# A hybrid decoder layer: the LRU's convolution one chunk ahead of its gates, and seven rotating PSUM banks instead of six

## The reference

```python
x = x + 0.5 * rms_norm(swiglu(rms_norm(x, g1), w_gu, w_down), g2)
y = hybrid_mixer(rms_norm(x, mix_pre_g), ...)
x = x + rms_norm(y, mix_post_g)
x = x + 0.5 * rms_norm(swiglu(rms_norm(x, g3), w_gu2, w_down2), g4)

# hybrid_mixer, the recurrent half (512 channels)
xc = causal_depthwise_conv(x_lru, conv_w, conv_b)        # width 4
r = sigmoid(block_diag(xc, w_rg, b_rg)); i = sigmoid(block_diag(xc, w_ig, b_ig))
log_a = 8.0 * r * log_sigmoid(lam); a = exp(log_a)
u = sqrt(-expm1(2 * log_a)) * (i * xc)
h[t] = a[t] * h[t-1] + u[t]
y_lru = h * gelu(gate_lru)
# the other half: attention over a window of 128 keys with a sink per head
y = concat([rms_norm(y_lru, g_lru_out), rms_norm(y_attn, g_attn_out)]) @ w_o
```

## Time and profile before

| | us |
|---|---|
| runs shown, median of 2 | 3468.2 (3390.47 and 3545.94) |
| profiled execution | 3390.16 |
| span of its slowest core, core 7 | 3388.6 |
| spans of all cores | 3377.7 to 3388.6 |
| PE busy, core 7 | 2952.9 (87%), 13,256 matmuls |
| DVE busy | 1545.5 (46%) |
| ACT busy | 1606.7 (47%) |
| mean granted TensorE clock, core 7 | 0.938 |

### The profile page before, as it was taken

The page is one execution under the profiler, slowest core; times in us unless marked ns, Lnnn a source line. Parts: engine busy times, 40 slices in busy tenths (PEclk is TensorE's granted clock), DMA queues, the critical chain, the costliest instruction groups (busy, mean ns, idle before and its releaser), DMA issues.

```text
span 3388.6 us, 41222 instructions; the slowest of 8 cores (3377.7 to 3388.6 us)
## 1 busy us (share of the span) xinstructions
PE 2952.9 (87%) x13256; PEld 1317.4 (39%) x13256; DVE 1545.5 (46%) x2378; ACT 1606.7 (47%) x2376; POOL 504.9 (15%) x744
## 2 busy tenths in 40 slices
PE   6999999999999999999989878777888986876887
PEld 3443444434444444444434323223344432332333
DVE  3255544545445455554555344444422245345252
ACT  3245454464555545555554455356322245445422
POOL 1111111111111111111111111111111110110110
PEclk9999999999999999999999988888899987987988
DMA  8998989899797987979889655565898974754785
GB/s 155 150 150 127 162 136 143 144 135 155 133 148 139 141 150 128 158 136 140 149 129 149 94 93 86 78 100 76 132 153 153 140 106 65 106 88 68 107 142 100
DMA packets 236335, 427.31 MB, mean 126 GB/s; under 512 B 13280, under 2 KB 95456, under 8 KB 236128
## 3 DMA queue, kind: packets, MB, share of 16 engines
q0 software_dynamic: 224320, 382.61, 74.7%
q1 hardware_dynamic: 11808, 42.07, 3.8%
HBM read 798.81 MB, written 8.39 MB: 238 GB/s over the span
## 4 chain that ended last, share of the span: by engine, by line
PE 64%; DVE 13%; ACT 13%; issue 5%; DMA 3%; DVEq 0%; ACTq 0%; SPq 0%; POOLq 0%
PE ps L120 62%; DVE s_y L370 2%; PE ps L124 2%; DVE s_hnm L339 2%; DMA s_xst<-xs 2%; ACT s_sq L301 2%; DVE s_dn L579 2%; DVE s_sg L399 1%; ACT L316 1%; ACT L486 1%; DVE s_xc L456 1%; ACT L397 1%; DVE s_xT L376 1%; DVE s_hseq L499 1%; DMA s_ring<-wgu 1%
## 5 line engine op out<-in xcount | busy, mean ns | idle before, releaser
L120 PE MATMUL ps<-s_hnf,s_ring 128*128 128x512 bf16 x7040 | 1642.6, 392 | 64.8 <-DVE s_hnf L339 35.7
L120 PEld LDWEIGHTS ps<-s_hnf,s_ring 128*128 128x128 bf16 x7040 | 702.7, 101 | 953.4 <-issue 206.4
L120 PE MATMUL ps<-s_act,s_ring 128*128 128x512 bf16 x3520 | 793.1, 382 | 4.1 <-DVE s_act L402 4.1
L399 DVE TENSOR_TENSOR s_sg<-ps,s_sg 128x512 f32<-128x512 f32 x440 | 302.8, 688 | 902.9 <-ACT s_sg L397 813.1
L289 POOL DMA_DIRECT2D s_ring<-wgu x440 | 308.8, 702 | 1590.4 <-PE ps L120 1404.0
L120 PEld LDWEIGHTS ps<-s_act,s_ring 128*128 128x128 bf16 x3520 | 346.1, 98 | 428.0 <-issue 21.1
L397 ACT ACTIVATE s_sg<-ps 128x512 f32<-128x512 f32 x440 | 260.1, 594 | 331.9 <-PE ps L120 295.0
L120 PE MATMUL ps<-s_hnm,s_ring 128*128 128x512 bf16 x1064 | 269.0, 402 | 96.3 <-DVE s_ycat L580 44.9
L402 DVE TENSOR_TENSOR s_act<-ps,s_sg 128x512 bf16<-128x512 f32 x440 | 304.3, 692 | 93.7 <-PE ps L120 62.9
L120 PE MATMUL ps<-s_sq,s_ones 128*128 128x512 bf16 x512 | 188.3, 410 | 105.4 <-ACT s_sq L301 53.3
L350 ACT ACTIVATE s_y<-ps 128x512 f32<-128x512 f32 x160 | 94.7, 592 | 332.0 <-PE ps L120 332.0
(11 more groups left out here) (84 smaller groups left out, 1822.8 us busy)
## 6 DMA issues: line engine op xcount, KB each, us to landing
s_ring<-wgu POOLq DMA_DIRECT2D x440, 512.0 KB, 7.1
s_ring<-wd POOLq DMA_DIRECT2D x160, 704.0 KB, 9.8
s_xst<-xs SPq DMA_DIRECT2D x64, 512.0 KB, 7.4
s_ring<-win POOLq DMA_DIRECT2D x106, 256.0 KB, 5.4
s_ring<-wo POOLq DMA_DIRECT2D x32, 256.0 KB, 4.9
out<-s_xst SPq DMA_DIRECT2D x16, 512.0 KB, 7.8
s_wgb<-wg POOLq DMA_DIRECT2D x1, 256.0 KB, 6.2
s_masks<-masks POOLq DMA_DIRECT2D x1, 96.0 KB, 8.2
```

Source lines behind the costliest of these rows:

```text
L120: return self.e.matmul(*a, **k)
L399: S.add("dve", lambda e, bg=bg, gi=gi: e.tensor_tensor(out=sg[gi][:], in0=ps[bg][:], in1=sg[gi][:], op=ALU.mult), reads=[("ps", bg), ("sg" ...
```

## The change

The LRU is taken apart into `lru_conv(c)` and `lru_gates(c)`. `s_xc` and `s_xcb` get two buffers each, used by even and odd chunks. The convolution and cast of chunk c+1, with its gate projection and Gelu in an output tile, are recorded one step before the gates of chunk c. `s_gl` goes: the Gelu is written straight into `s_ycat`, and the product with the scan is done in place. A chunk now has two steps of side instead of three in the warm-up, three instead of four in an output tile. The output projection no longer squares from PSUM and adds chunk by chunk in bank 6: after its eight copies ACT squares the eight chunks of `s_ycat` from SBUF in a row, and two steps later eight ones matmuls sum them in a rotating bank. Bank 6 joins the rotation: seven banks instead of six in the warm-up, three instead of two for side in the output tiles.

```diff
         def nb():
-            return 4 + nxt("sbank", 2) if bank_mode["split"] else nxt("bank", 6)
+            return 4 + nxt("sbank", 3) if bank_mode["split"] else nxt("bank", 7)
         def nbm():
-            return nxt("mbank", 4) if bank_mode["split"] else nxt("bank", 6)
+            return nxt("mbank", 4) if bank_mode["split"] else nxt("bank", 7)
...
-            for c in range(4):
-                yield from gen_lru_chunk(t, c, own, fl)
+            lru_conv(0, own)
+            yield
+            for c in range(4):
+                if c + 1 < 4:
+                    lru_conv(c + 1, own)
+                yield
+                if own:
+                    yield
+                lru_gates(t, c, own, fl)
+                yield
...
+        def lru_conv(c, own):
+            xc, xcb = xc2[c % 2], xcb2[c % 2]
...
             if own:
                 bgk = proj_chunk(4 + c)
-                S.add("act", lambda e: e.activation(out=gl[:], in_=ps[bgk][:], func=AF.Gelu),
-                      reads=[("ps", bgk)], writes=["gl"])
-            yield
-            yield
-            if own:
-                yield
+                S.add("act", lambda e: e.activation(out=ycat[:, c, :], in_=ps[bgk][:], func=AF.Gelu),
+                      reads=[("ps", bgk)], writes=[("ycat", c)])
+
+        def lru_gates(t, c, own, fl):
...
             yield
-            yield from gen_outproj(oproj, ycat, "ycat", SSB2, "s")
-            yield from gen_residual(par, ycat, "ycat", SSB2, 8, "gh1")
+            for m in range(8):
+                bk = oproj(m)
+                S.add("act", lambda e, m=m, bk=bk: e.activation(out=ycat[:, m, :], in_=ps[bk][:], func=AF.Copy),
+                      reads=[("ps", bk)], writes=[("ycat", m)])
+                yield
+            sis = sumsq_squares(lambda k: ycat[:, k, :], [("ycat", k) for k in range(8)], 8)
+            yield
+            yield
+            ri = sumsq_finish(sis, 1.0 / D)
+            yield from gen_residual(par, ycat, "ycat", None, 8, "gh1", ri=ri)
```

More of the change, by code:

```diff
@@ L186, in build_program @@
         xl = sb("xl", [128, 4, NT + 3], F32)
-        xc = sb("xc", [128, NT], F32)
-        xcb = sb("xcb", [128, NT], BF16)
+        xc2 = [sb("xc%d" % i, [128, NT], F32) for i in range(2)]
+        xcb2 = [sb("xcb%d" % i, [128, NT], BF16) for i in range(2)]
         r_t = sb("r_t", [128, NT], F32)
@@ L364, in gen_outproj, with gen_residual @@
             yield
-        def gen_residual(par, ybuf, ykey, ssb, ghcol, ghkey):
+        def gen_residual(par, ybuf, ykey, ssb, ghcol, ghkey, ri=None):
             xt = xT[par]
-            ri = finish_rstd(ssb, 1.0 / D)
+            if ri is None:
+                ri = finish_rstd(ssb, 1.0 / D)
             for k in range(8):
@@ L445, in gen_lru @@
                 yield
+            lru_conv(0, own)
+            yield
             for c in range(4):
-                yield from gen_lru_chunk(t, c, own, fl)
-        def gen_lru_chunk(t, c, own, fl):
+                if c + 1 < 4:
[7 more added lines that the diff above has]
+            xc, xcb = xc2[c % 2], xcb2[c % 2]
+            kx, kb_ = ("xc", c % 2), ("xcb", c % 2)
@@ L450, in gen_lru_chunk @@
             cw = lambda k: vec[:, V_CONVW + c * 4 + k:V_CONVW + c * 4 + k + 1]
-            S.add(CONV_ENG, lambda e: e.tensor_scalar(out=xc[:], in0=xl[:, c, 3:NT + 3], scalar1=cw(3),
+            S.add("dve", lambda e: e.tensor_scalar(out=xc[:], in0=xl[:, c, 3:NT + 3], scalar1=cw(3),
                                                    scalar2=vec[:, V_CONVB + c:V_CONVB + c + 1], op0=ALU.mult, op1=ALU.add),
-                  reads=[("xl", c), "vec"], writes=["xc"])
+                  reads=[("xl", c), "vec"], writes=[kx])
@@ L454, in gen_lru_chunk @@
             for k in range(3):
[L455 to L464, removed]
@@ L465, in gen_lru_chunk @@
-            S.add("act", lambda e: e.activation(out=xcb[:], in_=xc[:], func=AF.Copy), reads=["xc"], writes=["xcb"])
+                S.add("dve", lambda e, k=k: e.scalar_tensor_tensor(out=xc[:], in0=xl[:, c, k:k + NT], scalar=cw(k),
+                                                                  in1=xc[:], op0=ALU.mult, op1=ALU.add),
+                      reads=[("xl", c), "vec", kx], writes=[kx])
+            S.add("act", lambda e: e.activation(out=xcb[:], in_=xc[:], func=AF.Copy), reads=[kx], writes=[kb_])
@@ L493, in gen_lru_chunk @@
             S.add("dve", lambda e: e.tensor_tensor(out=i_t[:], in0=i_t[:], in1=xc[:], op=ALU.mult),
-                  reads=["i_t", "xc"], writes=["i_t"])
+                  reads=["i_t", kx], writes=["i_t"])
             S.add("dve", lambda e: e.tensor_tensor(out=i_t[:], in0=i_t[:], in1=m_t[:], op=ALU.mult),
@@ L504, in gen_lru_chunk @@
             if own:
-                S.add("dve", lambda e: e.tensor_tensor(out=ycat[:, c, :], in0=hseq[:], in1=gl[:], op=ALU.mult),
-                      reads=["hseq", "gl"], writes=[("ycat", c)])
-            yield
+                S.add("dve", lambda e: e.tensor_tensor(out=ycat[:, c, :], in0=ycat[:, c, :], in1=hseq[:], op=ALU.mult),
+                      reads=["hseq", ("ycat", c)], writes=[("ycat", c)])
         def gen_kv_proj():
```

9 lines of the change are left out of this document (5 added, 4 removed).

## The result

The changed kernel takes 3474.6 us in the median of 11 runs (3450.59 to 3752.28), the kernel before 3394.0 in 10 runs beside them (3387.11 to 3626.14). Some runs of either kernel are up to 300 us longer than the rest, so the medians carry part of that; the ratio, which leaves them out, is 1.0195 with an interval of [1.0172, 1.0217]: slower, by some 66 us. The profiled executions give 3453.06 against 3390.16, 62.9 more.

A forecast was written before the change was run, and what follows sets the result against it. PE was taken as busiest, held by latency in the in-order ACT and DVE queues and by waits for L580. From 3390.2 us, +121 (warm-up), -47 (output tiles) and -16 (output projection) gave 3448, range 3400 to 3500.

The forecast's parts named there:

- within: Whole kernel: time between 3322 and 3458 us, two per cent or 68 us either way; chance 0.52.
- slower: Whole kernel: time above 3458 us, from all of (2) and 0.24 of (1); chance 0.38.
- (1): Whole kernel: the sum holds at 3448 us, with its own range of 3415 to 3485; chance 0.66.
- (2): Output tiles give nothing because ACT is the chain, only the 16 at the ends stay: 3495 us; chance 0.14.
- The warm-up: 12 warm-up tiles: each loses 8.6 us by queue order plus 1.5 of clock, 10.1 a tile, +121 us.
- the chain: Warm-up LRU: ACT and DVE, in order, wait for each other in turn; slot 22's last product comes 9.00 us later.
- The clock term of 1.5: Warm-up tile: PE's clock falls after a wait of some 8 us, now exposed, adding 1.5 us a tile.
- the small waits: Warm-up tile: PE's two waits of 0.57 and 0.40 us after the cast's wait, said to vanish inside the chain.
- The output tiles: Mixer from first scores to third down projection: 125.04 us becomes 114.2, 11.7 gained four times, -47 us.
- The projection: Output projection, ends of stretches: residual and sum a step earlier, FFN norm squares wait less, -16 us, bounds 5 and 21.
- (3): Warm-up loss is hidden because DVE and ACT catch up beside the down projection: 3327 us; chance 0.12.
- (4): Faster: buffer and bank remove PE's waits, 3213 us, if slot 18's sigmoid is not held by chunk 1's cast; chance 0.08.

The follow-up runs named there:

- e2: Changed kernel with the 12 warm-up tiles back in the old order of three steps a chunk; ratio to the kernel before 0.9813, span 3329.5 us.
- e3: Changed kernel with, in the warm-up, only the cast of chunk c+1 moved behind the gates' last exp of chunk c; ratio to the kernel before 0.9817.
- e1: Changed kernel with steps, banks and output projection of before, leaving only the two buffers and the Gelu in place; ratio to the kernel before 1.0002.
- e6: Changed kernel with the old banks, six in the warm-up and two for side in output tiles; ratio to the kernel before 1.0223, span 3476.5 us.
- e9: Changed kernel with the old banks and old output projection, keeping new order, buffers and Gelu in place; no ratio on record, span 3475.6 us.
- e7: Changed kernel with the old LRU steps everywhere, keeping seven and three banks and the new output projection; ratio to the kernel before 0.9994.
- e5: Changed kernel with warm-up convolutions and gates spread over later steps and each later cast behind the previous gates' last exp; ratio to the kernel before 0.9602.
- run 16: Not a follow-up run: words of "then run 16 and 18 matmuls", the matmuls PE ran in two tiles of e7, 3.62 and 4.05 us.

## Why the prediction was right, and where it was wrong

**The step that failed** is "Two per cent, about what a measurement of this kernel can tell". The interval of the ratio is 0.45% wide from end to end, [1.0172, 1.0217], so a change of 1% would have been told from none. My sum stood at +58 us, 1.7%, and I split its case at 3458, ten us above my own number, which put 0.52 into "within" and only 0.38 into "slower": I forecast no change that a measurement could tell, and the runs show one of 1.95%, nine times the 0.22% that the interval reaches to either side. By the measurement's real width nearly all of cases (1) and (2), 0.80, was slower. The sum itself, 3448, stands 5 us below the profiled 3453.06; what failed is the bound by which I turned it into chances. It could have been doubted from the fact that the spans of all eight cores of one execution lie within 11 us, though that doesn't show how runs differ from each other.

**The warm-up: right, by the right cause.** L403 of slot 22 starts 39.50 us after that of slot 16 (898.47 less 858.97); the chain gave 39.22. From the end of convolution 0, 862.68 (L466 from 860.22 on, 2.46 long), to r of chunk 0, 869.61, are 6.9; it gave 7.0. L403 of slot 19 comes after 19.56 and that of slot 21 after 33.68; it gave 19.61 and 33.41. The wait at `d(1)` is 8.71 in this tile and 8.34 in most (forecast 8), 91.9 us in all (100), a tile 154.0 in the median (155), all 12 together +124.1, or +120.0 in the medians (+121). The clock term of 1.5 was too small: behind the eleven long waits the 26 matmuls take 7.35 to 8.73, 8.07 in the median, where they took 5.77, so 2.3 and in the tile shown 1.58. That the tile is only 9.7 longer and not 11 has a likely reason that I didn't follow up: before, PE waited for L402 in just 6 tiles, so in the others the chain had a little slack. e2 and e3 show that the place in the queues is the cause, e1 and e6 that neither buffers nor banks are.

**A detail of it: wrong.** I wrote that the small waits vanish inside the chain. PE's waits for L400 grew instead, from 26.5 to 68.6 us. They lie within the chain, so they don't move its end, which is why e6, with 136.6 us of them, has nearly the same tile (153.5).

**The output tiles: right in size, wrong in two links.** Forecast and measured: block 0 to 1, 29.2 and 30.2; 1 to 2, 27.9 and 27.9; 2 to 3, 21.0 and 20.9; block 3 to its P matmuls, 14.0 and 11.9; first scores to third `d`, 114.2 and 114.2. The first and the last of the four links miss by 1.0 and 2.1 and cancel in part; together they are 1.2 too long, and what follows them, 23.3 against my 22.1, is as much too short. That the total fits to the tenth is luck. The waits for L583 at blocks 1 and 2 are 7.88 and 8.33, as forecast. What I did not see is how the gain is made up, in the medians of the cores: the order alone brings 23 us (e1 to e9), the new projection at most 7 (e9 to e6), the third bank 28 (e6 to after). With the old order, bank and projection together bring nothing (e7). I had given the bank no share in my sum.

**The projection: size right, cause wrong.** The wait of 7.74 went to 2.08, the one of 2.61 went too, and all waits for L332 fell from 24.2 to 7.6 us, by the 16 that I wrote down. But I gave them to the new projection ("residual and sum are now a step earlier"). e7 has it and keeps a wait of 8.5; e9 doesn't and has none above 2.8 (10.3 us in all, against 24.2 in e1). The shorter LRU did it.

**The rivals.** (2), output tiles that give nothing, fell: -61.2, or -55.8 in the medians, against my -63. (3), a hidden loss, fell: +124.1. (4) fell for the change itself. Its condition was half of the matter: where the cast no longer holds slot 18's sigmoid (e3), the loss is gone, but none of the 5.4 us a tile that (4) wanted to gain comes; only with fewer convolutions ahead of the last product as well (e5) is a tile 6.4 us shorter than before. The Trainium skill ("Perfetto Trace Analysis", Optimization Strategy and Matmul Optimizations) takes repeated gaps as a hint of too few buffers and asks for all banks. The traces agree for the output tiles in the new order (e6 against after); in the old order the bank came together with the new projection and nothing was gained (e7). For the warm-up's gaps, the same in each of 12 tiles, they don't: e1 and e7 have more buffers and more banks, and ratios of 1.0002 and 0.9994.

**Open.** One warm-up tile of the changed kernel, the fifth, took 159.5 us where the others take 153.5 to 156.3. Leaving out the last one, the same tile is the longest in the traces of e2 to e7, by some 4 us over the median, and not in those of before, e1 and e9. PE's waits for a load of x are 43.1 us in 17 against 36.6 in 9 before, but 42.3 in e1 too. That these belong together, and what moves them from trace to trace, was not tried. Not run either: the third bank alone with the old order, and the spread order with one buffer.

## What to carry to other kernels

When a producer is moved ahead by a double buffer, write down what stands behind it on each in-order engine: if a consumer that waits for it (here a cast) stands in front of something that the busy engine needs sooner, running ahead makes the kernel slower. Here moving that one consumer back gave the whole loss back. Follow the chain to every next thing that the busy engine asks for, not to the first alone, or the wait only moves. And before adding a bank look at which bank is asked for next: two pairs of swapped allocations were worth some 20 us here, a seventh bank in the warm-up nothing.

## What the runs showed of the hardware

The clock falls behind some waits, and the wait's length doesn't tell whether, nor what it costs. 26 matmuls of the down projection take 5.77 us at full clock, and also in e6, where they follow a wait of 0.95. Behind the eleven long waits of the changed kernel, 7.80 to 8.71 us, they take 7.35 to 8.73; right behind the 8.71 the granted clock is 0.50 for 3 us (899.31 to 902.30), which is 1.2 GHz, and then 0.97. In e3 eleven waits of 3.75 to 4.10 are followed by 8.69 at most, by 7.46 in the median, and once, behind a wait of 3.75, by 5.77. In two tiles of e7 PE does the same work, one wait of 2.56 us follows, and the same 26 matmuls come out differently:

```profile
705.92 7.46 PE L120 MATMUL ps<-s_act,s_ring 128*128 128x512 bf16 x26 [2.56 <-DVE s_act L403]
...
851.84 5.77 PE L120 MATMUL ps<-s_act,s_ring 128*128 128x512 bf16 x26 [2.56 <-DVE s_act L403]
```

The granted clock is 0.77 over the first row and 1.00 over the second. In both PE had waited 3.03 or 3.04 us for a cast, then run 16 and 18 matmuls (3.62 and 4.05 us), then waited 2.56. Of the seven tiles of e7 with a wait of 2.55 to 2.57, three cost 1.69 us and four nothing, so the 1.7 us of one tile is no price to carry to the next. What makes the difference wasn't tried.
